# Router logits taken from the residual before it is normed, and the normed rows formed and turned later, in a two-block transformer kernel

## The chip, the cores and the metric

The kernel runs on one core of one Trainium2 chip. The metric is the device time of one execution in microseconds (us), the median of three runs. Engines are called by their names in the profile: PE (TensorE), DVE (VectorE), ACT (ScalarE), POOL (GpSimd) and SP (SyncE, which here only issues transfers).

## What is computed

Two blocks over 512 tokens of width 1024, in float32. The first block is a mixer with three branches, an output projection and a residual, and behind it a mixture of 16 experts in 4 groups. The change touches only the way from the residual to the experts:

```python
h = rms_norm(x, g_norm2) * (1.0 + sc2) + sh2
grp_prob = softmax(h @ w_group + b_group)          # 4 groups
p_g, g_idx = lax.top_k(grp_prob, 1)                # one group for each token
exp_logits = h @ w_router + b_router               # 16 experts
...                                                # two experts of that group, their weights
for gi in range(N_GROUPS):
    act = silu(h @ w_exp_gate[gi]) * (h @ w_exp_up[gi]) * combine[gi]
    y = y + act @ w_exp_down[gi]
```

`rms_norm` scales each token by one factor (rstd); `g_norm2`, `sc2` and `sh2` differ only from feature to feature.

## The kernel before, in words

Activations lie with the features on the 128 partitions and the 512 tokens along them, in KD = 8 blocks `k`. Every product is made exact enough by splitting both sides into a high part (float32r) and the rest: `three` issues the products high by high, low by high and high by low. ACT makes the high part of an activation (`hi_of`, semaphore `hi`), DVE the low part (`lo_of`, semaphore `lo`). Weights come in a stream of pieces of 1 MB, 16 tiles of 128 by 128: SP brings a piece into one of three `raw` slots, POOL splits it into `whi` and `wlo` in four parts, each one copy (L2482) and one difference (L2488), and PE multiplies with it. POOL may split a piece only when PE has ended with the piece two before it, and SP may load a piece only when the piece three before it is split.

The order of each engine is written out by hand in its block of `build`, and one engine waits for another by semaphores. Around the change the program goes:

- The output projection `wout` (4 pieces, 8 outputs). As each output k is ready, DVE adds it to the residual `X[:, k]` (L2059), ACT squares it, and DVE adds the squares up (`add_square`, L1739). PE sums them over the features (`norm_product`, L557), ACT makes `rstd` of it by Ln and Exp (L1231, L1233).
- DVE norms each block into `h2f` (L1755), ACT adds the shift and makes `hhi` (L1248), DVE makes `hlo` (L1725). PE multiplies each block with the router (20 columns: 4 groups and 16 experts, `rhi` and `rlo`), ACT copies the 20 by 512 logits out (`router_T`), PE turns them into tokens by logits (`routerT`, L808).
- DVE works through some 75 small operations on 4 to 80 columns: the group of each token (`grouped`), with the counts of the tokens of each group from PE (`counts`, L817), the order of the groups by size (`ranked`, L2112); then the two experts and their weights, with one Exp on ACT in between (`route_diff`, `route_exp`), the place of each token among those of its group (`places`, PE L822, which sums over the tokens before it), and four masks of 128 by 640 (`in_slot`, L2160). PE multiplies these masks in `slots_filled` (L875), turns the weights (`combT`, L881), and DVE copies them (L2167).
- SP waits for `ranked` before it loads the first expert piece (`moe0`), since the order of the groups says where in the stream it is. PE turns `h2f` into rows of tokens in 8 steps of 4 transposes (`h2_turned`, L801), which ACT copies into `h2_tok` and sends to memory, for a gather some time later.
- The largest group runs first, over all 512 tokens. Each expert has two pieces: `wide_first` multiplies the feature blocks 0 to 3 of it, `wide_second` the blocks 4 to 7. `slots_filled` stands between the two of the first expert. Behind them `expert_weight` spreads the token weights of the expert (L866), ACT copies them and DVE multiplies with them (L2173, L2175); the next expert's fourth PSUM bank comes free only by an operation behind that.

PSUM has 8 banks of 128 by 512. `open_bank` hands out the banks of a group (`main` has six of them, `out` two) in turn and makes PE wait for the reader of what last stood there; `share_banks` gives the groups other banks and starts them at their first.

## Time and profile before

| what | value |
|---|---|
| median of 3 runs | 1885.24 us (1879.75 to 1888.14) |
| the profiled execution, its own time | 1880.21 us |
| its span in the trace | 1878.3 us |
| PE busy, share of the span | 89% |
| POOL, DVE, ACT busy | 54%, 50%, 26% |
| mean granted clock of PE | 0.94 of full speed |

The page gives the busy time of each engine and the chain of waits that ended last. The span is counted from the first to the last instruction that the profiler saw; the time of the execution is 1.9 us longer. The stretch that the change touches lies between 652 us (the end of `wout` on PE) and 726 us (the start of the second expert). Rows of the timeline give the start and the duration of an instruction or of a run of equal ones, and in brackets how long its engine had been idle and what released it. A float32 product shows as two records.

### The profile page before, as it was taken

The page shows a single profiled execution, that of the slowest core. Times are in us where ns is not written, and L with a number is a line of the kernel's source. Part 1 is how long each engine was busy: PE and PEld are TensorE (multiplying, and loading weights), DVE is VectorE, ACT ScalarE, POOL GpSimd, SP SyncE. Part 2 cuts the span into 40 slices and gives each one's busy share as a digit, 9 for nine tenths or more (in the row PEclk, how much of TensorE's full clock was granted, in tenths as well). Part 3 has the DMA queues.
Part 4 walks back from the last instruction along what each step waited for, and adds up shares of the span by engine and source line. Part 5 has one row for each costly group of instructions (what it writes and reads, how often), then busy time and mean ns, then how long its engine had stood idle before and what let it go on. Part 6 is the DMA issues. An engine that isn't in the chain of part 4 may idle for free. (4 is left out here: it accounts for less than half of the span.)

```text
span 1878.3 us, 20749 instructions
## 1 busy us (share of the span) xinstructions
PE 1671.3 (89%) x7778; PEld 1311.7 (70%) x7778; DVE 930.4 (50%) x1437; ACT 496.5 (26%) x939; POOL 1012.1 (54%) x945
## 2 busy tenths in 40 slices
PE   4999798998979979999998699999897699999995
PEld 2778576776757757778876487666574578888884
DVE  7784654498773361231315861865457433133134
ACT  2201322313241121124444422433444420010011
POOL 2767553455717435757870345222374167777772
PEclk8999899998999978999999799998898799999997
DMA  9355211133212032314545532101121013223211
GB/s 362 141 199 197 98 67 68 56 112 113 90 68 90 1 135 93 143 68 157 191 152 187 212 101 90 45 24 45 46 90 68 23 68 105 97 90 112 91 68 45
DMA packets 32694, 197.54 MB, mean 105 GB/s; under 512 B 3735, under 2 KB 7591, under 8 KB 10964
## 3 DMA queue, kind: packets, MB, share of 16 engines
q1 hardware_dynamic: 26040, 179.57, 26.2%
q10 hardware_dynamic: 5836, 14.03, 2.2%
q0 software_dynamic: 720, 2.62, 0.4%
q8 instruction: 63, 1.03, 0.2%
q14 instruction: 35, 0.29, 0.0%
HBM read 190.90 MB, written 7.66 MB: 106 GB/s over the span
## 5 line engine op out<-in xcount | busy, mean ns | idle before, releaser
L2488 POOL TENSOR_TENSOR b_wlo<-b_raw,b_whi 128x512 fp32r<-128x512 f32 x516 | 705.5, 1375 | 70.5 <-ACT b_whi L1507 35.4
L2482 POOL TENSOR_SCALAR b_whi<-b_raw 128x512 fp32r<-128x512 f32 x420 | 312.1, 743 | 760.0 <-PE ps L436 578.2
L434 PE MATMUL ps<-b_hhi,b_whi 128*128 128x512 f32 (+1 forms) x1112 | 450.1, 405 | 27.4 <-POOL b_wlo L2488 8.0
L435 PE MATMUL ps<-b_hlo,b_whi 128*128 128x512 f32 (+1 forms) x1112 | 439.5, 395 | 0.0
L436 PE MATMUL ps<-b_hhi,b_wlo 128*128 128x512 f32 (+1 forms) x1112 | 438.6, 394 | 0.0
L434 PEld LDWEIGHTS ps<-b_hhi,b_whi 128*128 128x128 f32 x1112 | 213.6, 192 | 91.6 <-issue 45.0
L436 PEld LDWEIGHTS ps<-b_hhi,b_wlo 128*128 128x128 f32 x1112 | 213.5, 192 | 45.6
L435 PEld LDWEIGHTS ps<-b_hlo,b_whi 128*128 128x128 f32 x1112 | 213.9, 192 | 44.5 <-issue 2.4
L434 PE MATMUL ps<-b_ahi,b_whi 128*128 128x512 f32 x432 | 176.4, 408 | 12.5 <-DVE b_alo L1721 6.2
L435 PE MATMUL ps<-b_alo,b_whi 128*128 128x512 f32 x432 | 171.6, 397 | 0.0
L436 PE MATMUL ps<-b_ahi,b_wlo 128*128 128x512 f32 x432 | 171.2, 396 | 0.0
L434 PE MATMUL ps<-b_whi,b_hhi 128*128 128x512 f32 (+1 forms) x304 | 117.3, 386 | 14.0 <-DVE b_hlo L1725 5.0
L1255 ACT ACTIVATE b_arena<-ps 128x512 f32<-128x512 f32 (+6 forms) x102 | 54.0, 534 | 258.5 <-PE ps L436 188.5
L435 PE MATMUL ps<-b_wlo,b_hhi 128*128 128x512 f32 (+1 forms) x304 | 115.3, 379 | 0.0
L436 PE MATMUL ps<-b_whi,b_hlo 128*128 128x512 f32 (+1 forms) x304 | 115.3, 379 | 0.0
L434 PEld LDWEIGHTS ps<-b_ahi,b_whi 128*128 128x128 f32 x432 | 83.6, 193 | 39.0 <-DVE b_alo L1721 7.3
L1507 ACT ACTIVATE b_whi<-b_raw 128x512 fp32r<-128x512 f32 x144 | 78.8, 620 | 73.2 <-PE ps L436 70.7
L435 PEld LDWEIGHTS ps<-b_alo,b_whi 128*128 128x128 f32 x432 | 83.4, 193 | 17.9 <-issue 1.2
L436 PEld LDWEIGHTS ps<-b_ahi,b_wlo 128*128 128x128 f32 x432 | 83.1, 192 | 18.0
L434 PEld LDWEIGHTS ps<-b_whi,b_hhi 128*128 128x128 f32 x304 | 58.6, 193 | 25.9 <-issue 14.5
L1246 ACT ACTIVATE b_ahi<-b_arena 128x512 fp32r<-128x512 f32 x52 | 32.8, 632 | 144.1 <-DVE b_arena L2447 106.4
L1255 ACT ACTIVATE b_y<-ps 128x512 f32<-128x512 f32 (+4 forms) x62 | 40.3, 662 | 105.7 <-PE ps L763 91.4
(335 smaller groups left out, 2118.8 us busy)
## 6 DMA issues: line engine op xcount, KB each, us to landing
b_raw<-in_stream SPq DMA_DIRECT2D x165, 1024.0 KB, 4.8
bias_near<-bias_vectors ACTq DMA_DIRECT2D x1, 2298.0 KB
b_x<-in_xT SPq DMA_DIRECT2D x1, 2048.0 KB, 13.1
b_x<-in_xT ACTq DMA_DIRECT2D x1, 2048.0 KB, 7.7
h_tokens<-b_y ACTq DMA_DIRECT2D x1, 2048.0 KB, 11.8
b_arena<-in_cw ACTq DMA_DIRECT2D x1, 2048.0 KB, 7.3
out<-b_x SPq DMA_DIRECT2D x8, 256.0 KB, 2.0
bias_compressed<-bias_vectors ACTq DMA_DIRECT2D x1, 1024.0 KB
```

What stands on the lines that cost most here:

```text
L434: pe.matmul(o, ahi_, bhi_, start=start, stop=False)
L435: pe.matmul(o, ahi_, blo_, start=False, stop=False)
L436: return pe.matmul(o, alo_, bhi_, start=False, stop=stop)
L1246: run(nc.scalar.activation(dst, src, ACT.Copy, scale=gain), "hi")
L1255: run(nc.scalar.activation(dst, src, func, scale=scale, bias=bias), name)
L1507: run(nc.scalar.activation(whi[:, n % SPLIT_SLOTS, c], raw[:, i % RAW_SLOTS, c], ACT.Copy), "moe_hi")
L2482: nc.gpsimd.tensor_scalar(whi[:, s, c], raw[:, r, c], 1.0, 1.0, ALU.mult, ALU.mult)\
L2488: nc.gpsimd.tensor_tensor(wlo[:, s, c], raw[:, r, c], whi[:, s, c].bitcast(F32), ALU.subtract)\
```

## The change

The router's product is linear, and rstd is one factor for a token. So the logits are (X times gain, through the router) times rstd, plus the router's product with the shift `sh2`, which is the same for all tokens. With this:

- `hi_of("route", k)` and `lo_of("route", k)` split X times gain into `ahi` and `alo` as soon as output k of `wout` is added to X, ahead of the squares; PE runs seven of the eight router steps behind `wout`, then the sum of squares, then the eighth. DVE multiplies the logits by rstd as it takes them out of PSUM. `gain` and three small tables are made before the loop.
- The shift's part of the logits is made once, before the attention of the first block: 16 products of one column (`shift`), a diagonal of it by DVE (`route_bias`), and a second product in each of four `routerT` steps adds it.
- DVE does the small operations up to `ranked` and the places first, and then `h2_formed`: the norming and splitting that stood ahead of the router, and the counting table. The choice of experts follows behind it.
- `h2_turned` for the features 0 to 511 of all four token tiles stands ahead of the first piece, for the features 512 to 1023 behind `wide_first`, and `slots_filled` behind `wide_second`. The first piece waits for the low parts of `h2` by blocks. The banks are shared out accordingly. The Exp for `route_diff` stands on ACT behind the last copy of the turned rows.

```diff
@@ -113,3 +113,3 @@
-SPLITS, NSPLITS = offsets({"h1": 8, "ya": 4, "yb": 4, "yc": 4, "merged": 8, "h2": 8,
+SPLITS, NSPLITS = offsets({"h1": 8, "ya": 4, "yb": 4, "yc": 4, "merged": 8, "route": 8, "h2": 8,
                            "moe0": 8, "n0": 8, "conv": 4, "nsa": 4,
@@ -241,2 +241,3 @@
         rout = ar(2560, 512)
+        route_bias = small[0:20, 480:500]
         combT = arena[0:4, 0:512]
@@ -778,2 +779,9 @@
             linear(("gate", 2), range(3), KD, hhi, hlo, 0, "gate_read")
+            pe.wait_ge(sem("router_split"), 1)
+            o = open_bank("shift", "shift_read")
+            for k in range(KD):
+                for n, w in enumerate((rhi, rlo)):
+                    ins = pe.matmul(o[0:20, 0:1], w[:, k, :].bitcast(F32), mod[:, 24 + k:25 + k],
+                                    start=k + n == 0, stop=k + n == KD)
+            mark(ins, "shift")
             pe.wait_ge(sem("rstd_used"), 1 + 4 + 8)
@@ -786,15 +794,19 @@
             linear("wout", range(KD), KD, hhi, hlo, 0, "wout_read", "merged")
+            share_banks(side=[6, 7])
+            logits = open_bank("router", "router_T", "side")
+            def route_step(k):
-            norm_product("sum_h2", KD)
+                pe.wait_ge(sem("lo"), SPLITS["route"] + k + 1)
+                return three(logits[0:20, :], rhi[:, k, :], rlo[:, k, :], ahi[:, k, :], alo[:, k, :],
+                             k == 0, k == KD - 1)
-            o = open_bank("router", "router_T")
-            pe.wait_ge(sem("router_split"), 1)
-            for k in range(KD):
-                pe.wait_ge(sem("lo"), SPLITS["h2"] + k + 1)
-                ins = three(o[0:20, :], rhi[:, k, :], rlo[:, k, :], hhi[:, k, :], hlo[:, k, :], k == 0, k == KD - 1)
-            mark(ins, "router")
+            for k in range(KD - 1):
+                route_step(k)
+            norm_product("sum_h2", KD)
+            mark(route_step(KD - 1), "router")
+            share_banks(main=[0, 1, 2, 3], turned=[4, 5, 6, 7])
             def h2_turned(T, half):
-                o = open_bank(("h2_tok", T, half), "h2_tok")
+                o = open_bank(("h2_tok", T, half), "h2_tok", "turned")
                 for k in range(4):
@@ -803,11 +815,9 @@
-            h2_turned(0, 0)
             pe.wait_ge(sem("router_T"), 1)
+            pe.wait_ge(sem("route_bias"), 1)
             o = open_bank("routerT", "router_read")
             for T in range(ST):
-                ins = pe.transpose(o[:, T * 32:T * 32 + 20], rout[0:20, T * P:(T + 1) * P], ident[0:20, 0:20])
+                pe.matmul(o[:, T * 32:T * 32 + 20], rout[0:20, T * P:(T + 1) * P], ident[0:20, 0:20], start=True, stop=False)
+                ins = pe.matmul(o[:, T * 32:T * 32 + 20], ones[0:20, :], route_bias, start=False, stop=True)
             mark(ins, "routerT")
-            h2_turned(0, 1)
-            h2_turned(1, 0)
-            h2_turned(1, 1)
             goh = small[:, 464:480].rearrange("p (a n) -> p a n", a=ST)
@@ -824,6 +834,5 @@
             mark(ins, "places")
-            for T in range(2, ST):
+            for T in range(ST):
+                pe.wait_ge(sem("lo"), SPLITS["h2"] + 4)
                 h2_turned(T, 0)
-                h2_turned(T, 1)
-            share_banks(turned=[6, 7])
@@ -871,3 +880,3 @@
                 pe.wait_ge(sem("in_slot"), ST)
-                o = open_bank("slots", "slots_known")
+                o = open_bank("slots", "slots_known", "turned")
                 for b in range(5):
@@ -878,3 +887,3 @@
                 pe.wait_ge(sem("combined"), 1)
-                o = open_bank("combT", "combT_read")
+                o = open_bank("combT", "combT_read", "turned")
                 for T in range(ST):
@@ -885,7 +894,11 @@
                 keys = [(("eg", e), 0), (("eg", e), 1), (("eu", e), 0), (("eu", e), 1)]
-                o = wide_first(keys, hhi, hlo, ["silu_read"] * 2 + ["eu_read"] * 2)
+                o = wide_first(keys, hhi, hlo, ["silu_read"] * 2 + ["eu_read"] * 2, None if e else "h2")
                 if e == 0:
-                    slots_filled()
+                    for T in range(ST):
+                        pe.wait_ge(sem("lo"), SPLITS["h2"] + KD)
+                        h2_turned(T, 1)
                 wide_second(o, keys, hhi, hlo)
                 if e == 0:
+                    slots_filled()
+                    share_banks(main=[4, 5, 0, 1, 2, 3], turned=[6, 7])
                     pe.wait_ge(sem("combT_read"), 1)
@@ -1470,8 +1483,5 @@
             for k in range(KD):
-                act.wait_ge(sem("wout_read"), k + 1)
+                hi_of("route", k, ahi[:, k, :], src=X[:, k, :], ready=("wout_read", k + 1), gain=gain[:, k:k + 1])
                 square_for("sum_h2", k, X[:, k, :])
             rstd_of("sum_h2", D)
-            for k in range(KD):
-                hi_of("h2", k, hhi[:, k, :], src=h2f[:, k, :], bias=mod[:, 24 + k:25 + k])
-            evacuate("router", rout[0:20, :], "router_T", src=ps[0:20, bank_of["router"], :])
             act.wait_ge(sem("route_max"), 1)
@@ -1479,8 +1489,14 @@
             run(nc.scalar.activation(gl_e, gl_e, ACT.Exp), "route_exp")
+            def h2_turned(T, half):
+                evacuate(("h2_tok", T, half), h2_tok[:, T, half * 512:(half + 1) * 512], "h2_tok")
+
+            for k in range(KD):
+                hi_of("h2", k, hhi[:, k, :], src=h2f[:, k, :], bias=mod[:, 24 + k:25 + k])
+                if k in (5, 7):
+                    h2_turned(k - 5, 0)
+                    h2_turned(k - 4, 0)
             for T in range(ST):
-                for half in range(2):
-                    evacuate(("h2_tok", T, half), h2_tok[:, T, half * 512:(half + 1) * 512], "h2_tok")
-                if T == 1:
-                    act.wait_ge(sem("route_diff"), 1)
-                    run(nc.scalar.activation(stat[:, 8:12], stat[:, 8:12], ACT.Exp), "route_exp")
+                h2_turned(T, 1)
+            act.wait_ge(sem("route_diff"), 1)
+            run(nc.scalar.activation(stat[:, 8:12], stat[:, 8:12], ACT.Exp), "route_exp")
             act.wait_ge(sem("h2_tok"), 2 * ST)
@@ -2038,2 +2054,6 @@
+            finished(dve, "shift")
+            run(V.tensor_scalar(route_bias, ident[0:20, 0:20], ps[0:20, bank_of["shift"], 0:1], None, ALU.mult),
+                "route_bias")
+            run(V.memset(small[:, 362:363], 0.0), "shift_read")
             dve.wait_ge(sem("bias1_in"), 16 * 4)
@@ -2056,2 +2076,8 @@
             dve.wait_ge(sem("x_in"), 32)
+            run(V.scalar_tensor_tensor(gain[:, :], mod[:, 32:40], 1.0, col("g2", 0, 8), op0=ALU.add, op1=ALU.mult))
+            run(V.tensor_tensor_scan(group4, ones[:, 0:1].to_broadcast([P, 4]), ones[:, 0:1].to_broadcast([P, 4]),
+                                     0.0, ALU.mult, ALU.add))
+            run(V.tensor_scalar(ranks4, group4, -1.0, None, ALU.add))
+            run(V.tensor_scalar(tie4, group4, -1.0, 4.0, ALU.mult, ALU.add))
+            run(V.tensor_scalar(first_w, group4, -1.0, 5.0, ALU.mult, ALU.add))
             for k in range(KD):
@@ -2060,18 +2086,22 @@
                                            op0=ALU.mult, op1=ALU.add), "wout_read")
-                add_squares_behind("sum_h2", k)
-            run(V.scalar_tensor_tensor(gain[:, :], mod[:, 32:40], 1.0, col("g2", 0, 8), op0=ALU.add, op1=ALU.mult))
+                if k >= 2:
+                    add_square("sum_h2", k - 1)
+                lo_of("route", k, alo[:, k, :], ahi[:, k, :], X[:, k, :], gain=gain[:, k:k + 1])
+            add_square("sum_h2", KD - 1)
             wait_rstd()
-            h2_normed = normed(KD, lambda k: X[:, k, :], lambda k: gain[:, k:k + 1])
-            for k in range(KD + 1):
-                if k < KD:
-                    h2_normed(k, h2f[:, k, :])
-                if k:
-                    lo_of("h2", k - 1, hlo[:, k - 1, :], hhi[:, k - 1, :], h2f[:, k - 1, :], mod[:, 23 + k:24 + k])
-            run(V.tensor_tensor_scan(count_up, ones[:, 0:1].to_broadcast([P, SLOTS]), ones[:, 0:1].to_broadcast([P, SLOTS]),
-                                     0.0, ALU.mult, ALU.add))
-            run(V.tensor_tensor(tmp[0][:, 0:P], ident, count_up[:, 0:P], ALU.mult))
-            run(V.tensor_reduce(tok1, tmp[0][:, 0:P], AX.X, ALU.add))
-            run(V.tensor_scalar(ranks4, count_up[:, 0:4], -1.0, None, ALU.add))
-            run(V.tensor_scalar(tie4, count_up[:, 0:4], -1.0, 4.0, ALU.mult, ALU.add))
-            run(V.tensor_scalar(first_w, count_up[:, 0:4], -1.0, 5.0, ALU.mult, ALU.add))
+            finished(dve, "router")
+            run(V.tensor_tensor(rout[0:20, :], ps[0:20, bank_of["router"], :], rstd[0:20, :], ALU.mult), "router_T")
+
+            def h2_formed():
+
+                h2_normed = normed(KD, lambda k: X[:, k, :], lambda k: gain[:, k:k + 1])
+                for k in range(KD + 1):
+                    if k < KD:
+                        h2_normed(k, h2f[:, k, :])
+                    if k:
+                        lo_of("h2", k - 1, hlo[:, k - 1, :], hhi[:, k - 1, :], h2f[:, k - 1, :], mod[:, 23 + k:24 + k])
+                run(V.tensor_tensor_scan(count_up, ones[:, 0:1].to_broadcast([P, SLOTS]), ones[:, 0:1].to_broadcast([P, SLOTS]),
+                                         0.0, ALU.mult, ALU.add))
+                run(V.tensor_tensor(tmp[0][:, 0:P], ident, count_up[:, 0:P], ALU.mult))
+                run(V.tensor_reduce(tok1, tmp[0][:, 0:P], AX.X, ALU.add))
@@ -2112,2 +2142,6 @@
             run(V.tensor_scalar(group_at[:, :], group4, float(MOE_PIECES), None, ALU.mult), "ranked")
+            finished(dve, "places")
+            run(V.tensor_tensor(t16, goh, tiles(bank("places", 16), ST), ALU.mult), "places_read")
+            run(V.tensor_reduce(place_of, t16, AX.X, ALU.add))
+            h2_formed()
@@ -2149,5 +2183,2 @@
             run(V.tensor_reduce(rank_of, t16, AX.X, ALU.add))
-            finished(dve, "places")
-            run(V.tensor_tensor(t16, goh, tiles(bank("places", 16), ST), ALU.mult), "places_read")
-            run(V.tensor_reduce(place_of, t16, AX.X, ALU.add))
             run(V.tensor_scalar(slot_of, rank_of, -1.0, 256.0, ALU.add, ALU.mult))
```

On PE, from the end of `wout` to the first expert piece, before (`b_con` holds the unit matrix, `b_small` the routing values, `b_arena` the squares, `h2f` and the logits):

```order
L436 MATMUL ps<-b_hhi,b_wlo 128x512
L557 MATMUL ps<-b_arena,b_con 128x512 [waits s_wout_read,s_squares_added]
L434 MATMUL ps<-b_hhi,b_rhi 20x512 [waits s_lo,s_router_split,s_wout_read]
...
L808 MATMUL ps<-b_con,b_arena 128x20 [waits s_wout_read,s_router_T]
...
L817 MATMUL ps<-b_small,b_con 128x4 [waits s_router_T,s_grouped]
...
L822 MATMUL ps<-b_small,b_con 128x4 [waits s_h2_tok]
...
L434 MATMUL ps<-b_hhi,b_whi 128x512 [waits s_h2_tok,s_weights_split,s_places_read,s_counts_read]
```

and now (lines of the changed kernel):

```order
L437 MATMUL ps<-b_hhi,b_wlo 128x512
L435 MATMUL ps<-b_ahi,b_rhi 20x512 [waits s_lo,s_dsa_out_read]
...
L558 MATMUL ps<-b_arena,b_con 128x512 [waits s_wout_read,s_squares_added]
...
L820 MATMUL ps<-b_con,b_arena 128x20 [waits s_wout_read,s_route_bias,s_router_T]
L821 MATMUL ps<-b_small,b_con 128x20
...
L827 MATMUL ps<-b_small,b_con 128x4 [waits s_wout_read,s_grouped]
...
L832 MATMUL ps<-b_small,b_con 128x4 [waits s_wout_read]
...
L813 MATMUL ps<-b_con,b_arena 128x128 [waits s_mean_square_read,s_lo]
...
L435 MATMUL ps<-b_hhi,b_whi 128x512 [waits s_places_read,s_weights_split,s_counts_read,s_lo,s_router_read,s_wout_read]
```

The router's steps moved ahead of the sum of squares, and the norming is waited for only by the transposes (L813) and the first piece.

On DVE, around `ranked`, before:

```order
L2112 TENSOR_SCALAR b_group_at<-b_small 128x4 [waits s_dve_step]
L2126 TENSOR_TENSOR b_small<-b_small 128x16 [waits s_ranked]
L2126 TENSOR_TENSOR b_small<-b_small 128x16 [waits s_dve_step]
L2129 TENSOR_TENSOR b_small<-b_small 128x16 [waits s_dve_step]
L2126 TENSOR_TENSOR b_small<-b_small 128x16 [waits s_dve_step]
```

and now:

```order
L2142 TENSOR_SCALAR b_group_at<-b_small 128x4 [waits s_dve_step]
L2144 TENSOR_TENSOR b_small<-b_small,ps 128x16 [waits s_matmuls_done,s_ranked]
L2145 TENSOR_REDUCE b_small<-b_small 128x4 [waits s_places_read]
L1771 SCALAR_TENSOR_TENSOR b_arena<-b_x,b_gain,b_arena 128x512 [waits s_dve_step]
...
L1741 SCALAR_TENSOR_TENSOR b_hlo<-b_arena,b_mod,b_hhi 128x512 [waits s_hi,s_lo]
L2103 SCALAR_TENSOR_TENSOR b_arena<-b_con 128x640 [waits s_lo]
L2105 TENSOR_TENSOR b_arena<-b_con,b_arena 128x128 [waits s_dve_step]
L2106 TENSOR_REDUCE b_small<-b_arena 128x1 [waits s_dve_step]
L2160 TENSOR_TENSOR b_small<-b_small 128x16 [waits s_dve_step] x2
```

Eight norming and eight low-part operations, the table and two small ones now stand between `ranked` and the choice of experts.

## Rows read from the trace of the kernel before

**Rows 1.** The page's busy times: busy us, share, instructions.

```profile
PE 1671.3 (89%) x7778; PEld 1311.7 (70%) x7778; DVE 930.4 (50%) x1437; ACT 496.5 (26%) x939; POOL 1012.1 (54%) x945
```

**Rows 2.** Timeline of PE, 651 to 726 us: start, duration, instruction, idle before.

```profile
651.40 0.39 PE L435 MATMUL ps<-b_hlo,b_whi 128*128 128x512 f32 x1
651.62 0.39 PE L436 MATMUL ps<-b_hhi,b_wlo 128*128 128x512 f32 x1
655.52 2.08 PE L557 MATMUL ps<-b_arena,b_con 128*128 128x512 f32 x2 [3.51 <-DVE b_arena L1739]
...
673.76 1.53 PE L801 MATMUL ps<-b_con,b_arena 128*128 128x128 f32 x12
676.69 1.05 PE L817 MATMUL ps<-b_small,b_con 128*128 128x4 f32 x8 [1.40 <-DVE b_small L2094]
677.60 3.78 PE L822 MATMUL ps<-b_small,b_con 128*128 128x4 f32 x20
681.24 3.65 PE L801 MATMUL ps<-b_con,b_arena 128*128 128x128 f32 x16
689.34 0.77 PE L434 MATMUL ps<-b_hhi,b_whi 128*128 128x512 f32 x1 [4.44 <-POOL b_wlo L2488]
...
703.18 6.30 PE L875 MATMUL ps<-b_small,b_arena 128*128 128x5 f32 x40
...
722.25 1.12 PE L866 MATMUL ps<-b_arena,b_con 4*128 4x512 f32 x2
725.93 0.62 PE L434 MATMUL ps<-b_hhi,b_whi 128*128 128x512 f32 x1 [2.57 <-DVE b_arena L2173]
```

**Rows 3.** Windows: PE, PEld, DVE, ACT, POOL busy (count), granted PE clock, DMA share, GB/s.

```profile
689.00:703.00 14.00, 13.66 (x48) 11.04 (x49) 7.08 (x9) 0.00 (x0) 13.42 (x15) 0.77 0.83 298
```

**Rows 4.** Timeline of DVE, 659 to 711 us.

```profile
659.08 1.54 DVE L1755 SCALAR_TENSOR_TENSOR b_arena<-b_x,b_gain,b_arena 128x512 f32<-128x512 f32 x2 [3.42 <-ACT b_arena L1233]
...
671.84 1.49 DVE L2070 TENSOR_TENSOR_SCAN b_arena<-b_con 128x640 f32<-128x640 f32 x1
...
674.63 0.24 DVE L2082 TENSOR_TENSOR b_small<-ps,b_small 128x80 f32<-128x80 f32 x1
...
679.09 0.17 DVE L2112 TENSOR_SCALAR b_group_at<-b_small 128x4 int32<-128x4 f32 x1
...
684.59 0.16 DVE L2138 TENSOR_TENSOR b_small<-b_small 128x4 f32<-128x4 f32 x1
...
687.36 0.51 DVE L2153 TENSOR_SCALAR b_small<-b_small 128x4 f32<-128x4 f32 x1
...
690.05 4.58 DVE L2160 TENSOR_SCALAR b_arena<-b_arena,b_small 128x640 f32<-128x640 f32 x4
...
710.46 0.68 DVE L2167 COPY b_arena<-ps 4x512 f32<-4x512 f32 x1 [0.47 <-PE ps L881]
```

**Rows 5.** Timeline of POOL: the first part of the first expert piece, and the next.

```profile
687.22 0.62 POOL L2482 TENSOR_SCALAR b_whi<-b_raw 128x512 fp32r<-128x512 f32 x1 [48.05 <-DMA b_raw<-in_stream]
...
689.16 0.61 POOL L2482 TENSOR_SCALAR b_whi<-b_raw 128x512 fp32r<-128x512 f32 x1
```

**Rows 6.** Timeline of DVE at 40 us, the first norming, while POOL splits.

```profile
40.70 0.98 DVE L1755 SCALAR_TENSOR_TENSOR b_arena<-b_x,b_gain,b_arena 128x512 f32<-128x512 f32 x1
41.71 1.65 DVE L1725 SCALAR_TENSOR_TENSOR b_hlo<-b_arena,b_mod,b_hhi 128x512 fp32r<-128x512 f32 x1
43.40 0.99 DVE L1755 SCALAR_TENSOR_TENSOR b_arena<-b_x,b_gain,b_arena 128x512 f32<-128x512 f32 x1
```

**Rows 7.** Timelines around the start of the first attention, and products of one column.

```profile
426.62 0.95 PE L566 MATMUL ps<-b_con,b_x 128*128 128x1 f32 x8
432.70 1.87 PE L566 MATMUL ps<-b_con,b_x 128*128 128x1 f32 x8 [5.13 <-DVE b_x L1780]
...
514.20 1.05 PE L768 MATMUL ps<-b_arena 128*128 128x128 f32 x8
...
519.10 0.29 DVE L2023 SCALAR_TENSOR_TENSOR b_x<-ps,b_x 128x128 f32<-128x128 f32 x1
```

4 lines of the change are left out of this document (2 added, 2 removed).

## The prediction

> **What bounds the kernel now.** I read the page first: PE is busy 89% of the span [rows 1], so the kernel is PE's work plus the holes in it, and a change pays only in a hole. Then the timeline of PE around the change. There the reader sees a stretch with little work: the output projection ends at 651.62 + 0.39 = 652.0 us, the first expert piece starts at 689.34, and what ended the last wait is POOL's split of that piece [rows 2]. POOL in turn was released by the transfer at 687.22 after 48 us without work [rows 5], and SP could ask for the transfer only after `ranked`, which DVE finished at 679.09 + 0.17 = 679.26 [rows 4]. So the chain is: projection, squares, rstd, norming, router, small operations, `ranked`, 7.96 us to the landed piece, 2 us for its first part. Behind it come a first piece at a low clock (granted mean 0.77, so partly at 1.2 instead of 2.4 GHz [rows 3]) and the slots, before which DVE stood idle for long. That last wait is the one to watch: the change gives DVE more to do ahead of the slots.
>
> **The start of the first attention.** The shift product adds 16 products of one column, 32 records. Eight such records with 128 weight columns took 0.95 us right behind dense work and 1.87 us after an idle spell [rows 7], so 3.8 to 7.5 us; these have 20 weight columns, and I take the lower end, since they follow dense work. PE has room: its first logits were issued at 514.20, and DVE first read them at 519.10 [rows 7]. 514.2 + 3.8 = 518.0, and the first logits behind them still come in time. DVE does two small operations more there, 0.35 us, with nothing beside them, so **+0.35**; at the upper end of 7.5 us logits come at about 522, **+3**.
>
> **Up to `ranked`.** The splits of X times gain (for each output one more operation of some 0.78 us on DVE and one on ACT) lie in waits for the projection; without that cover each pair would cost some 1.5. The last of them delays the last addition of squares by nothing: DVE waited there for ACT's square. PE now has 21 router products first, at the 0.22 us of the projection's own rows [rows 2]: 652.0 + 4.7 = 656.7, past 655.52, where the sum of squares started. In return that product meets a warm PE and takes half of its 2.08 us: 657.75 against 657.60 before (658.8 if it is cold). DVE follows 1.48 us behind as before, 659.25; taking out the logits costs what the copy of 4 by 512 costs, 0.68 us [rows 4]; `routerT` is now 16 records at 0.13 (1.05 / 8) to 0.19 us (3.78 / 20) [rows 2], 2.1 to 3.0, say 2.5. DVE gets the logits at 662.6, not at 674.63. From there to `ranked` the work is unchanged, 679.26 - 674.63 = 4.63: **667.2, 12.0 us earlier**. The first piece lands at 667.2 + 7.96 = 675.2.
>
> **What comes behind it now.** DVE waits for the places (PE ends them 681.38 - 674.63 = 6.75 us behind the logits, at 669.4), does two small operations and starts the norming at 669.8. Up to 675.2 it does seven of the 16 operations, 0.78 us each [rows 4]. Then POOL is splitting, and the price of the same pair of operations is in the first norming of the kernel, where POOL was splitting too: 0.98 + 1.65, a pair every 2.70 us [rows 6]. The fourth low part is ready at 677.9, the eighth at 675.2 + 4.5 x 2.7 = 687.4, the table (1.49 [rows 4]) and its two followers at 689.8. PE turns the first halves, 16 transposes in 3.65 us, until 681.6; the first piece takes 703.18 - 689.34 = 13.8 us as before, until 695.4; the second halves cost 1.53 x 16 / 12 = 2.0, until 697.5; the second piece, without the slow start it had, 48 records at 0.225, until **708.3**. There the slots follow. Before they followed the first piece at 703.18.
>
> **DVE's way to the slots.** From 689.8 on it has 27 small operations to the Exp, of which 25 read two operands or are plain scalings, then 14 more, then the masks. Undisturbed one takes (684.59 - 679.09) / 28 = 0.20 us; with POOL splitting, five took 690.05 - 687.36 = 2.69, so 0.54 each [rows 4]. POOL ends its first two pieces at about 694.2 (4.5 parts at 2.7, 3.5 at 1.94 [rows 5]), starts the third at 695.4, when PE is done with the first, and ends it at 703.2. So: 8 operations to 694.2, 6 in the gap, 11 at 0.54 to 701.3, the rest to 701.7; the Exp, behind ACT's last copy, at 702.2; the 14 to 705.6. The masks took 4.58 us while POOL was splitting [rows 4]; POOL now idles until PE ends the second piece at 708.3. No row shows them undisturbed. Upper end 4.58, so 710.2; the lower end is that of the like-sized table step with more work in it, some 0.6 each (1.49 is a running sum over 640), so 708.0. I take the middle, **709.3**: DVE arrives 1 us behind PE.
>
> The Trainium skill (SBUF — State Buffer, § Who interferes with whom) says that a DVE instruction with two SBUF inputs contends with a GpSimd instruction that reads SBUF, and that the one issued second "fully blocks" until the first is done. Read strictly, each small operation waits out a POOL instruction of its own (0.97 us); the row above shows more than one slipping through (0.54). The sum would then be that of rival 2.
>
> **The sum.** From the slots' start to DVE's copy of the weights took 711.14 - 703.18 = 7.96 us, and the spreading product follows 0.1 later: 709.3 + 8.1 = 717.4, and 0.9 more if PE is slow after its wait (0.19 against 0.16 us for 40 records), 718.3, against 722.25: -4.0. The wait of 3.68 us behind it (722.25 to 725.93) stays: the fourth bank again needs DVE's second operation; POOL is idle there, -0.2. PE comes out of a longer sparse stretch into the second expert; the first piece after such a stretch lost (13.8 - 10.8) = 3 us, this one lost less, so +0.6. With the attention: -4.0 - 0.2 + 0.6 + 0.35 = **-3.2 us**. The rest of the program only shifts. Against the profiled execution, 1880.21, that is 1877.0; that execution lies 5 us under the median, so against the median of 1885.24 it gives **1882.0**. A measurement of this kernel tells about 0.5%, 9.4 us, from no change; the three runs before span 8.4 us.
>
> **Rivals.**
> 1. PE ends last, DVE is early (less meeting with POOL, masks at 0.6 each): slots at 708.3 and not slow, -5.9 - 0.2 + 0.6 + 0.35 = -5.1, 1880.1. For it: the masks meet an idle POOL. Against it: 25 of 27 operations of the kind that waited in rows 4. If the first piece also starts warm, 3 us more on PE, DVE again decides.
> 2. DVE waits out a whole POOL instruction each time: 4.5 + 6 + 8 operations by 703.2, the rest free, 705; masks at 708.2 to 712.8, and the spreading product at 721.8: -0.5 + 0.75 = +0.3, 1885.5.
> 3. **Slower**: PE's clock stays at 1.2 GHz through both pieces, because transposes and waits now break up its work three times before the slots. 48 records then cost 20.5 us each time, twice the 0.225: 681.6 + 20.5 + 3.65 + 20.5 = 726.2 and the spreading product at 735: +13, 1898. It decides from about 9 us more of low clock than the 6 us before (each such us loses half). Against it: before, the first piece lost only 3 us to it, right behind just such a sparse stretch.
> 4. The shift products do not fit before the attention: +3 instead of +0.35, 1884.7.
> 5. The routing does not come earlier (the sum of squares or the logits wait for something I missed): only the costs are left, about 1886.
>
> **Numbers.** Forecast 0.40, rival 1 0.25, rival 2 0.14, rival 3 0.05, rival 4 0.08, rival 5 0.08. Faster by over 0.5% needs rival 1 with a warm start and masks in time, or scatter of the runs: 0.09. Slower by over 0.5% is rival 3 nearly alone: 0.04. The rest, 0.87, is within 0.5%. The range takes in the forecast and rivals 1, 2, 4 and 5 with the scatter of a median: 1875 to 1889.
>
> **What would show it.** Right: `ranked` near 667, POOL's first part near 675, norming operations of 1.0 and 1.65 us on DVE, the first expert piece on PE near 682, a wait of about 1 us for DVE's masks ahead of the slots, the spreading product near 718. Wrong: `ranked` later than 671 (rival 5), DVE's masks done before PE's second piece (rival 1) or 4 us behind it (rival 2), a granted clock near 0.5 from 682 to 708 (rival 3), DVE idle ahead of its first attention operation (rival 4).

## The result, and the profile after

| | before | changed |
|---|---|---|
| median of nine runs each | 1885.24 us (1879.75 to 1888.8) | 1892.43 us (1884.3 to 1896.88) |
| ratio to before, 95% interval | | 1.0042 (1.0025 to 1.0059) |
| the profiled execution, its own time | 1880.21 us | 1884.3 us |
| its span | 1878.3 us | 1882.1 us |

The change makes the kernel slower, by 0.42% (4.7 to 11.1 us by the interval). That is still inside the 0.5% that I called no change, but it is measured, it has the other sign than the forecast of -3.2 us, and the median lies outside the range of 1875 to 1889.

The page of the changed kernel, which answers to [rows 1]:

```profile
span 1882.1 us, 20872 instructions
...
PE 1670.1 (89%) x7822; PEld 1316.3 (70%) x7822; DVE 950.7 (51%) x1449; ACT 501.6 (27%) x946; POOL 1016.0 (54%) x945
```

The busy times hardly differ, so the loss is in idle time and order. The timeline of PE over the same stretch, answering to [rows 2]:

```profile
656.33 1.02 PE L558 MATMUL ps<-b_arena,b_con 128*128 128x512 f32 x2
...
664.44 1.87 PE L827 MATMUL ps<-b_small,b_con 128*128 128x4 f32 x8 [2.17 <-DVE b_small L2124]
666.17 4.41 PE L832 MATMUL ps<-b_small,b_con 128*128 128x4 f32 x20
679.70 3.68 PE L813 MATMUL ps<-b_con,b_arena 128*128 128x128 f32 x16 [9.12 <-DVE b_hlo L1741]
683.02 0.78 PE L435 MATMUL ps<-b_hhi,b_whi 128*128 128x512 f32 x1
...
694.70 1.91 PE L813 MATMUL ps<-b_con,b_arena 128*128 128x128 f32 x16
...
707.15 0.39 PE L437 MATMUL ps<-b_hhi,b_wlo 128*128 128x512 f32 x1
715.12 8.70 PE L884 MATMUL ps<-b_small,b_arena 128*128 128x5 f32 x40 [7.59 <-DVE b_arena L2191]
723.68 1.01 PE L890 MATMUL ps<-b_con,b_small 128*4 128x128 f32 x4
725.53 2.07 PE L875 MATMUL ps<-b_arena,b_con 4*128 4x512 f32 x2 [0.84 <-DVE b_arena L2198]
730.01 0.76 PE L435 MATMUL ps<-b_hhi,b_whi 128*128 128x512 f32 x1 [2.41 <-DVE b_arena L2204]
```

The row at 715.12 is the one to see. PE ended the second piece at 707.5 (forecast: 708.3) and then stood 7.59 us for DVE's masks; before, the slots had no wait at all. The windows (columns: PE busy, granted clock, DMA share, GB/s) show the second part of the price:

```profile
683.00:697.00 14.00, 14.00 (x69) 0.95 0.23 75
697.00:715.00 18.00, 10.54 (x47) 0.91 0.60 234
715.00:730.00 15.00, 11.64 (x46) 0.50 0.18 70
```

Behind that wait the granted clock is 0.50, the lower level of 1.2 GHz. The first piece and the turns behind it in return run at 0.95, against 0.77 for the first piece in [rows 3]. The timeline of DVE, answering to [rows 4]:

```profile
667.66 0.17 DVE L2142 TENSOR_SCALAR b_group_at<-b_small 128x4 int32<-128x4 f32 x1
670.69 0.17 DVE L2144 TENSOR_TENSOR b_small<-b_small,ps 128x16 f32<-128x16 f32 x1 [2.86 <-PE ps L832]
...
671.10 1.54 DVE L1771 SCALAR_TENSOR_TENSOR b_arena<-b_x,b_gain,b_arena 128x512 f32<-128x512 f32 x2
...
678.66 0.98 DVE L1741 SCALAR_TENSOR_TENSOR b_hlo<-b_arena,b_mod,b_hhi 128x512 fp32r<-128x512 f32 x1
679.68 1.65 DVE L1771 SCALAR_TENSOR_TENSOR b_arena<-b_x,b_gain,b_arena 128x512 f32<-128x512 f32 x1
...
689.50 1.78 DVE L2103 TENSOR_TENSOR_SCAN b_arena<-b_con 128x640 f32<-128x640 f32 x1
...
695.26 1.14 DVE L2160 TENSOR_TENSOR b_small<-b_small 128x16 f32<-128x16 f32 x1
696.44 0.54 DVE L2163 TENSOR_TENSOR b_small<-b_small 128x16 f32<-128x16 f32 x1
697.02 0.17 DVE L2166 TENSOR_REDUCE b_small<-b_small 128x4 f32<-128x16 f32 x1
...
706.20 0.17 DVE L2175 TENSOR_SCALAR b_small<-b_small 128x4 f32<-128x4 f32 x1 [0.34 <-ACT b_small L1501]
...
708.57 1.11 DVE L2186 SCALAR_TENSOR_TENSOR b_small<-b_small 128x4 f32<-128x4 f32 x1
709.72 0.56 DVE L2187 TENSOR_SCALAR b_small<-b_small 128x4 f32<-128x4 f32 x1
710.31 0.17 DVE L2188 COPY b_small<-b_small 128x16 f32<-128x16 f32 x1
710.52 4.54 DVE L2191 TENSOR_SCALAR b_arena<-b_arena,b_small 128x640 f32<-128x640 f32 x4
```

And that of POOL, answering to [rows 5]: the first part of the first piece, parts of the third (696.34) and the fourth piece (from 707.70).

```profile
675.80 0.62 POOL L2513 TENSOR_SCALAR b_whi<-b_raw 128x512 fp32r<-128x512 f32 x1 [36.37 <-DMA b_raw<-in_stream]
...
695.08 1.29 POOL L2519 TENSOR_TENSOR b_wlo<-b_raw,b_whi 128x512 fp32r<-128x512 f32 x1
696.34 0.62 POOL L2513 TENSOR_SCALAR b_whi<-b_raw 128x512 fp32r<-128x512 f32 x1
697.04 1.30 POOL L2519 TENSOR_TENSOR b_wlo<-b_raw,b_whi 128x512 fp32r<-128x512 f32 x1
...
707.70 0.62 POOL L2513 TENSOR_SCALAR b_whi<-b_raw 128x512 fp32r<-128x512 f32 x1 [3.48 <-PE ps L437]
708.40 1.26 POOL L2519 TENSOR_TENSOR b_wlo<-b_raw,b_whi 128x512 fp32r<-128x512 f32 x1
```

Read the two together at 695 to 697. The small operation of 1.14 us ends with POOL's difference (695.08 + 1.29), the next, of 0.54, with POOL's copy (696.34 + 0.62), and the third takes its bare 0.17. A POOL part of 1.96 us lets three of DVE's small operations pass. The same meeting stretches the masks at 710.52 to 1.14 us each: POOL could start its fourth piece at 707.70, because PE had just ended with the second.

So the 11.4 us that `ranked` came earlier (667.83 against 679.26) shrink to 6.3 at the first piece (683.0 against 689.34), because the forming of h2 now stands behind `ranked` and meets POOL from 675.80 on, and turn into a loss of 4.1 at the second expert (730.01 against 725.93).

### The profile page after: what moved, and what is told of

The parts are those of the page before. It is cut to its first block and busy times, and to the rows that moved or that the text cites. A ratio compares the mean times of both kernels' runs of the same rounds, so it can differ in the third digit from the quotient of the medians.

```text
span 1882.1 us, 20872 instructions
## 1 busy us (share of the span) xinstructions
PE 1670.1 (89%) x7822; PEld 1316.3 (70%) x7822; DVE 950.7 (51%) x1449; ACT 501.6 (27%) x946; POOL 1016.0 (54%) x945
## 5 line engine op out<-in xcount | busy, mean ns | idle before, releaser
L435 PE MATMUL ps<-b_whi,b_hhi 128*128 128x512 f32 (+1 forms) x304 | 116.9, 384 | 13.4 <-DVE b_hlo L1741 5.3
L1268 ACT ACTIVATE b_arena<-ps 128x512 f32<-128x512 f32 (+5 forms) x101 | 53.3, 534 | 243.2 <-PE ps L437 160.2
```

Source lines behind the costliest of these rows:

```text
L435: pe.matmul(o, ahi_, bhi_, start=start, stop=False)
L1268: run(nc.scalar.activation(dst, src, func, scale=scale, bias=bias), name)
```

## The experiments

Single executions of one kernel scatter by some 15 us here, and much of that arises long before the stretch in question. The thirteen traces fall into two groups: in seven the granted clock between 300 and 350 us is 0.93 and `wout` ends at 650 to 652 us (the early group), in six the clock there is 0.66 to 0.69 and `wout` ends at 661 to 667 (the late group). So each run is given in two ways: by its ratio to the kernel before, and by landmarks of its trace, in us behind the end of `wout` on PE (651.6 us in the changed kernel, 652.0 before). "Spreading" is the product L875 (before: L866) of the first expert, "second spreading" that of the second expert, "end" the end of the trace.

| kernel | `ranked` | first piece | masks start | slots | spreading | second expert | second spreading | end | ratio (95%) |
|---|---|---|---|---|---|---|---|---|---|
| before | 27.2 | 37.3 | 38.0 | 51.2 | 70.2 | 73.9 | 97.5 | 1226.3 | 1 |
| forecast for the change | 15.2 | 29.6 | 53.6 | 57.3 | 66.3 | 69.8 | | | 0.998 |
| changed | 16.2 | 31.4 | 58.9 | 63.5 | 73.9 | 78.4 | 103.0 | 1230.5 | 1.0042 (1.0025 to 1.0059) |
| c1 changed, again | 15.9 | 30.7 | 58.7 | 63.3 | 73.7 | 78.2 | 103.0 | 1229.8 | 1.0036 (1.0016 to 1.0057) |
| c2 fourth piece held | 16.1 | 31.3 | 57.4 | 59.8 | 69.8 | 74.3 | 97.7 | 1222.7 | 1.0026 (1.0010 to 1.0041) |
| c3 third piece held | 16.1 | 31.4 | 52.2 | 55.7 | 61.9 | 66.4 | 90.3 | 1220.2 | 0.9979 (0.9957 to 1.0001) |
| c11 c3 again | 16.0 | 31.1 | 52.0 | 55.7 | 61.7 | 66.2 | 90.2 | 1219.5 | 0.9969 (0.9953 to 0.9985) |
| c4 filler products | 15.9 | 31.0 | 58.9 | 63.5 | 70.5 | 75.0 | 99.8 | 1227.3 | 1.0004 (0.9979 to 1.0028) |
| c5 c3 and banks | 16.0 | 30.9 | 52.2 | 55.5 | 61.8 | 63.8 | 87.4 | 1216.0 | 0.9953 (0.9931 to 0.9975) |
| c10 c5 again | 16.1 | 31.3 | 52.2 | 55.8 | 62.0 | 64.0 | 87.4 | 1216.0 | 0.9948 (0.9925 to 0.9971) |
| c6 c5, first piece held | 16.0 | 29.7 | 52.4 | 55.1 | 61.4 | 63.4 | 87.2 | 1215.7 | 0.9978 (0.9956 to 0.9999) |
| c7 choice first | 16.0 | 47.0 | 60.0 | 70.6 | 77.8 | 82.3 | 106.8 | 1236.4 | 1.0064 (1.0036 to 1.0092) |
| c8 slots between | 16.0 | 31.2 | 57.2 | 59.6 | 82.3 | 86.0 | 108.0 | 1232.9 | 1.0077 (1.0048 to 1.0106) |
| c9 before, banks | 27.2 | 37.4 | 38.1 | 51.2 | 70.3 | 71.4 | 93.3 | 1222.6 | 0.9989 (0.9972 to 1.0007) |

c1 to c4 ran on one chip, c5 to c8 on one, c9 to c11 on one, each with its own runs of the kernel before. The landmarks and the end repeat to 0.7 us or better (changed and c1, c3 and c11, c5 and c10), although each of these pairs has one trace from each group. The end can differ by some 4 us from what the second spreading product promises: c2 has that product 0.2 us behind the kernel before, and its end 3.6 us ahead. The ratios depend as well on how many executions fall into which group, and c2's says 0.26% slower. A few us in a ratio alone, or in one landmark alone, carry no weight below.

**c1: the changed kernel once more.**

> The changed kernel once more, as the control of the others on the same chip. Both theories: 0.3 to 0.6% slower than before, PE idle for 6 to 9 us ahead of the slots, the slots' 40 records at 0.19 to 0.23 us each.

It measured 1.0036 (1.0016 to 1.0057), with a wait of 7.58 us and 0.22 us a record, and the landmarks stand. The slowdown is real.

**c2 and c3: POOL held back.** One line in POOL's block makes it wait for the four masks before it splits a piece, the fourth in c2 (`MOE_AT + 3`), the third in c3 (`MOE_AT + 2`):

```diff
+                if i == MOE_AT + 3:
+                    pool.wait_ge(sem("in_slot"), ST)
                 if rank == 0:
                     pool.wait_ge(sem(f"raw_in{r}"), 16 * (i // RAW_SLOTS + 1))
```

> The changed kernel with POOL held off the fourth expert piece until the four masks are made. Theory A (DVE is late at the slots because its operations meet POOL's split): the masks take 0.6 us each instead of 1.14, the five small operations ahead of them 0.2 instead of 0.5, and the slots start near 711.5 instead of 715.1, so 3 to 4 us off the changed kernel. Theory B (the loss comes from what was added ahead of the slots, whatever POOL does): the slots start within 1 us of 715. Theory C (the loss is PE's clock, which the sparse stretch lets fall): the start may move, but the time moves by less than 1.5 us.

> The changed kernel with POOL held off the third and the fourth expert piece until the masks are made. Theory A: from 695 us on DVE works alone, its remaining small operations take 0.2 us each, the masks are ready at 705 to 706, ahead of PE's second piece (707.4), the slots start at 707.5, the spreading product near 716, and the kernel is 8 to 12 us faster than the changed one and 3 to 6 us faster than before. The third piece is then split at about 713, in time for the second expert. Theory B: no gain. Theory C: a gain of at most what the wait was at low clock, 4 us.

The masks (DVE) and the slots and what follows (PE) in c2's timeline:

```profile
708.88 2.32 DVE L2191 TENSOR_SCALAR b_arena<-b_arena,b_small 128x640 f32<-128x640 f32 x4
```

```profile
711.25 8.31 PE L884 MATMUL ps<-b_small,b_arena 128*128 128x5 f32 x40 [3.88 <-DVE b_arena L2191]
```

and in c3's:

```profile
702.94 2.32 DVE L2191 TENSOR_SCALAR b_arena<-b_arena,b_small 128x640 f32<-128x640 f32 x4
```

```profile
706.45 4.52 PE L884 MATMUL ps<-b_small,b_arena 128*128 128x5 f32 x40
710.83 0.95 PE L890 MATMUL ps<-b_con,b_small 128*4 128x128 f32 x4
712.62 2.07 PE L875 MATMUL ps<-b_arena,b_con 4*128 4x512 f32 x2 [0.84 <-DVE b_arena L2198]
```

With POOL quiet a mask takes 0.58 us instead of 1.14. Holding the fourth piece brings the slots 3.7 us forward, holding the third 7.8. PE then doesn't wait for them, its granted clock is still 0.99 during them, and 40 slot products take 4.52 us instead of 8.70. The second expert comes 12.0 us earlier than in the changed kernel, and the end 10.3, with the same work done. By the ratios c3 is 0.57% faster than c1, while c2's ratio (1.0026) can't be told from c1's. That carries the theory that DVE comes late because its operations meet POOL's, and speaks against a loss from the added work as such. The Trainium skill (SBUF — State Buffer, § Who interferes with whom) names both kinds of DVE instruction that contend with GpSimd, those with two SBUF inputs and `tensor_scalar` in a 2-port mode; the masks are `tensor_scalar`, and 0.58 against 1.14 us agrees that they contend; no run shows the mode that they ran in.

**c4: is it the clock?** 30 needless products on PE fill its wait for the masks (the first of the added waits makes sure that bank 7 has been read):

```diff
+                pe.wait_ge(sem("h2_tok"), 2 * ST)
+                for n in range(30):
+                    pe.matmul(ps[:, 7, :], hhi[:, n % KD, 0:P], hhi[:, n % KD, :], start=True, stop=True)
                 pe.wait_ge(sem("in_slot"), ST)
```

> The changed kernel with 30 needless products of 128 by 512 ahead of the wait for the masks, so that PE works through 6.5 of its 7.6 idle us; they write a free PSUM bank and leave the result alone. Theory A: the start of the slots stays at 715; what is won is the clock alone, 40 records at 0.16 instead of 0.22 us (2.4 us) and a warmer start of the second expert (up to 1.7 us), so 2 to 4 us faster than the changed kernel. Theory C (the clock is the whole loss): 7 us or more, as fast as before or faster. If the clock plays no part: within 1 us of the changed kernel.

```profile
718.25 6.96 PE L882 MATMUL ps<-b_hhi 128*128 128x512 f32 x30
726.10 5.28 PE L887 MATMUL ps<-b_small,b_arena 128*128 128x5 f32 x40 [0.89 <-DVE b_arena L2194]
731.24 1.01 PE L893 MATMUL ps<-b_con,b_small 128*4 128x128 f32 x4
```

The slots come as late as in the changed kernel (63.5), but take 5.28 us instead of 8.70, so the way from them to the spreading product falls from 10.4 to 7.0 us. The second expert comes 3.4 us earlier and the end 3.2. So the low clock behind the wait is worth 3.4 us of the change's loss, as theory A had it; the 7.6 us of the wait itself stay.

**c5: the hole behind the spreading product.** c3 still waits 2.48 us for DVE ahead of the second expert. c5 is c3 with another order of banks:

```diff
-                    share_banks(main=[4, 5, 0, 1, 2, 3], turned=[6, 7])
+                    share_banks(main=[4, 5, 3, 0, 1, 2], turned=[6, 7])
```

> The changed kernel with POOL held back before the third expert piece until the masks are written (as in c3), and with the six banks behind the slots handed out as 4, 5, 3, 0, 1, 2 instead of 4, 5, 0, 1, 2, 3, so that the fourth bank of the second expert is one that DVE reads with its first operation (L2204), not its second. c3's trace shows 712.62 for the spreading product, 2.07 us of it, and 717.16 for the second expert with a wait of 2.48 us that ended with DVE's second L2204. Theory E (that wait is only the order in which banks come free): the second expert starts about 2.0 to 2.5 us earlier against the end of the output projection, some 64 instead of 66.4, and keeps the gain at the spreading product of its second weight (some 88 instead of 90.3); ratio to the kernel before about 0.9967. Rival F (the second expert then waits elsewhere: for another bank that ACT reads, or its pieces come late because POOL was held back): the start or the next spreading product stays where c3 has it, ratio 0.998. If the clock of PE also stays up for want of the gap, 1 us more: c3 shows 1.6 times the usual duration for some 4 us behind the gap.

The second expert follows right behind the product, 2.0 us after its start, at 63.8, where theory E wanted some 64. The clock did not stay up: the next products take 0.63 us a record, as in c3.

```profile
722.78 2.07 PE L875 MATMUL ps<-b_arena,b_con 4*128 4x512 f32 x2 [1.21 <-DVE b_arena L2198]
724.79 0.80 PE L435 MATMUL ps<-b_hhi,b_whi 128*128 128x512 f32 x1
725.38 0.63 PE L436 MATMUL ps<-b_hlo,b_whi 128*128 128x512 f32 x1
```

**c6: the first piece held too**, until the fourth low part of h2 is ready.

```diff
+                if i == MOE_AT:
+                    pool.wait_ge(sem("lo"), SPLITS["h2"] + 4)
```

> c5 with one wait more: POOL starts the first expert piece only when DVE has made the fourth low part of h2. In the changed kernel POOL starts at 675.80, while DVE forms h2 at 2.70 us a pair, and the first half turn on PE waits 9.12 us for DVE, until 679.70; the piece is wanted at 683. Theory A (meeting POOL is what slows DVE here too): the fourth low part comes about 1 us earlier, at 15 to 16 us behind ranked less that, PE's first half turns and its first piece start 0.5 to 1 us earlier, since POOL's first part (1.95 to 2.7 us) is then ready about when the turns end; the end gains up to 1 us over c5. Rival G: POOL's first part comes late instead (DVE's fifth and sixth block meet it all the same), and PE waits for POOL at the first piece: first piece later by up to 1 us, the end the same or worse. I hold G for as likely as A here: what is at stake is 1 us either way.

The fourth low part comes at 26.4 instead of 27.5 us (c5), the first piece 1.2 us earlier than in c5, the second expert 0.4, the end 0.3. So theory A's mechanism is there, and little of it reaches the end. The ratio is higher than c5's, 0.9978 against 0.9953, with intervals that overlap; in its profiled run `wout` ends at 666.9 us against c5's 661.0, ahead of anything that differs. Differences of 0.3 to 0.4 us are below what the pairs above repeat to, so whether anything remains is open.

**c7: the choice of experts ahead of the forming.** `h2_formed()` is called behind the computation of `slot_of`, and ACT's second Exp stands ahead of its `hi_of("h2", ...)`.

```diff
             run(V.tensor_reduce(place_of, t16, AX.X, ALU.add))
-            h2_formed()
...
             run(V.scalar_tensor_tensor(slot_of, rank_of, 0.0, slot_of, op0=ALU.is_gt, op1=ALU.mult))
+            h2_formed()
```

> The changed kernel with DVE's choice of the two experts and their weights (some 40 small operations) moved from behind the forming of h2 to ahead of it, and ACT's second Exp likewise; POOL is not held back. Before the first piece lands, POOL is idle, and the small operations then take 0.2 us instead of 0.54 to 0.65, some 8 to 9 us in all. The forming then starts near 680 instead of 671, under POOL from its start: fourth low part about 691, so PE's first piece starts some 8 us later against the end of the projection (39 to 41 instead of 31.4), the first piece ends at 54, and the slots follow the second piece at 67 to 68 with no wait for the masks. Theory A (it is DVE's operations under POOL that come late, and the order of DVE's work decides which engine pays): PE waits at the first piece instead of at the slots, the second expert starts at 77 to 80 (after: 78.4), and the ratio is within 0.2% of the changed kernel's. Rival H (the place of the wait matters: with the wait ahead of the first piece PE runs both pieces and the slots without a break at full clock): second expert at 74 to 76, ratio about 0.2% below the changed kernel's.

The wait did move to the first piece, and grew. DVE's timeline shows the price of a small operation without POOL and with it:

```profile
682.04 0.17 DVE L2151 TENSOR_SCALAR b_small<-b_small 128x4 f32<-128x4 f32 x1
682.24 0.17 DVE L2153 TENSOR_TENSOR b_small<-b_small 128x4 f32<-128x4 f32 x1
...
689.65 1.12 DVE L2179 TENSOR_TENSOR b_small<-b_small 128x16 f32<-128x16 f32 x1
690.81 0.54 DVE L2180 TENSOR_TENSOR b_small<-b_small 128x16 f32<-128x16 f32 x1
```

and PE's the wait:

```profile
704.86 3.29 PE L813 MATMUL ps<-b_con,b_arena 128*128 128x128 f32 x16 [25.21 <-DVE b_hlo L1741]
```

POOL began at 684.91, before the choice was through, and the forming, from 693.51 on, met it from its start: first piece at 47.0, not at 39 to 41, second expert 3.9 us later than in the changed kernel (82.3, where theory A wanted 77 to 80 and rival H 74 to 76). As an order this one loses. One half of rival H came true all the same: with the wait ahead of the first piece, PE went from that piece to the second expert in 35.3 us, as in c3 (35.0) and not in the changed kernel's 47.0. What cost the time is that the first piece came 15.6 us later, more than the 11.7 gained behind it. Whether a wait of equal length would be cheaper there was not tested.

**c8: one part undone.** The slots stand between the two pieces again, as before the change.

```diff
+                if e == 0:
+                    slots_filled()
                 wide_second(o, keys, hhi, hlo)
                 if e == 0:
-                    slots_filled()
```

> The changed kernel with the slots back where they stood before, behind the first piece (and the second half turns) and ahead of the second piece: one part of the change undone. The masks can't be ready for it: PE stands at the slots from about 697.5. POOL then can't start the fourth piece, since PE still has the second piece to do, so DVE's last operations and the masks meet only the third piece, which POOL ends near 704. Theory A: the masks are done at about 709 to 710 instead of 715.1, the slots run at a low clock behind a wait of 12 us until 719, the second piece takes 11 to 14 us behind them, and the second expert starts at 83 to 85 behind the end of the projection (after: 78.4): slower than the changed kernel by 5 to 7 us, ratio to the kernel before 1.006 to 1.008. Rival B (the loss was in moving the slots, not in DVE's lateness): second expert at or before 76, ratio at or below 1.001.

```profile
711.69 8.70 PE L884 MATMUL ps<-b_small,b_arena 128*128 128x5 f32 x40 [14.60 <-DVE b_arena L2192]
```

PE waits 14.60 us there, twice as long as in the changed kernel, and the second expert comes 7.6 us later, a little more than expected (86.0 against 83 to 85); at the end 2.4 us of it are left. With the choice of experts behind the forming, moving the slots back was right. The masks end at 59.5, and not at 63.4, since POOL has no fourth piece to split, as in c2.

**c9: the bank order on the kernel before**, for what is left of early routing.

```diff
                 if e == 0:
+                    first4 = [bank_of[key] for key in keys]
+                    share_banks(main=[bank_of["slots"], bank_of["combT"]] + first4)
                     pe.wait_ge(sem("combT_read"), 1)
```

> The kernel before with only the order of banks of c5: from the spreading product on, main hands out the bank of the slots, the bank of the turned weights and then the four of the first expert, so that the second expert's fourth bank needs only DVE's first operation. In the kernel before PE waited 2.57 us there (722.25 spreading product, 725.93 second expert). Theory E (that hole is a matter of bank order in either kernel): the second expert starts near 71.5 behind the end of the output projection instead of 73.9, ratio about 0.9987. Theory E alone would then leave c5 (63.8) some 7 to 8 us ahead of this kernel, and that is what early routing is worth once POOL is held back. Rival F (the hole is filled by another wait): second expert at 73 or later, ratio 1.000.

```profile
720.42 1.12 PE L866 MATMUL ps<-b_arena,b_con 4*128 4x512 f32 x2
743.45 1.12 PE L866 MATMUL ps<-b_arena,b_con 4*128 4x512 f32 x2
```

The hole closes in this kernel too (71.4 instead of 73.9; 23.0 us from one spreading product to the next). The ratio of 0.9989 alone can't be told from 1. POOL was not held back in the kernel before; its slots have no wait for DVE that this could shorten (703.18 in [rows 2]).

**c10 and c11: c5 and c3 again, on c9's chip.**

> c5 once more, on the chip of c9, so that the two can be set side by side. Landmarks as in c5: masks 52.2, slots 55.5, spreading product 61.8, second expert 63.8 behind the end of the projection; that is 10.1 us ahead of the kernel before at the second expert, so a ratio near 0.9947; c5 measured 0.9953. Against c9 7 to 8 us, 0.4%.

> c3 once more, on the chip of c9 and c10. By its landmarks (second expert at 66.4, 7.5 us ahead of the kernel before) the ratio should be 0.9960; c3 measured 0.9979 with an interval of 0.9957 to 1.0001. If the landmarks are what counts, this one falls between c9 and c10, some 2.5 us behind c10; if it comes out at 0.998 again, some 4 us of what the landmarks show are lost in a part of the program that I have not looked at.

Medians on that chip: before 1883.98, c9 1881.48, c11 1877.04, c10 1870.8 us. The order is that of the landmarks. c11 measured 0.9969, between the 0.9960 of its landmarks and the 0.998 of the other reading, and lies 6.2 us behind c10 in the medians, 3.5 us at the end and 2.2 at the second expert. c10 beats the kernel before by 0.52% (0.29 to 0.75%) and c9 by 10.7 us in the medians, 7.7 us by the two ratios, 7.4 us at the second expert, 6.6 us at the end. So early routing is worth some 7 us, once POOL keeps out of DVE's way; in the change as made that worth was spent on a wait.

## Why the prediction was wrong

**Up to the second piece it held**, to within 2 us or so. `ranked` 667.83 (667.2), POOL's first part 675.80 (675.2), norming operations of 1.65 and 0.98 us, first piece at 683.0 (681.6), end of the second piece at 707.5 (708.3). The last match has luck in it: the first piece began 1.4 us late and took 11.7 us instead of the 13.8 "as before", at a granted clock of 0.95. The counts and places ran slower, 0.23 us a record against [rows 2]'s 0.13 and 0.19, which made the forming start 1.3 us late. The shift product cost nothing that shows: DVE's first attention operation starts at 519.02, against 519.10 in [rows 7]. The trace of the changed kernel has its 32 records in a microsecond, and attention begins 0.5 us behind [rows 7]'s 514.20, still well ahead of DVE:

```profile
513.81 0.21 PE L784 MATMUL ps<-b_mod,b_rhi 128*20 128x1 f32 x2
...
514.58 0.19 PE L784 MATMUL ps<-b_mod,b_rlo 128*20 128x1 f32 x2
514.70 1.16 PE L769 MATMUL ps<-b_arena 128*128 128x128 f32 x8
```

My 3.8 us came from products with 128 weight columns and was too high by a factor of four. Rivals 4 and 5 are out, and so is rival 3: the stretch from 683 to 697 ran at 0.95, the next, with the second piece, at 0.91.

**The step that failed is "DVE's way to the slots".** It put the end of the masks at 709.3; they ended at 715.06, 5.8 us later. By its own terms:

| term | forecast | measured | late by |
|---|---|---|---|
| table done (places, forming, scan) | 689.8 | 692.83 | 3.0 |
| 27 small operations and the Exp | 12.4 us | 13.4 us (to 706.20) | 1.0 |
| 14 operations to the masks | 3.4 us | 4.3 us (to 710.52) | 0.9 |
| the masks | 3.7 us | 4.5 us | 0.8 |

The first two, 4.0 us together, are mis-sized. Of the 3.0 us, 1.3 are the late start of the forming, 0.8 the forming itself and 1.0 the table, whose operations POOL stretched (1.78 us for the running sum, 1.49 in [rows 4]). Of the small operations each cost 0.65 us under POOL, where five rows of [rows 4] gave 0.54, and the gap of 1.2 us between POOL's second and third piece, in which six of them were to run at 0.2, didn't come: POOL ended the second piece at 696.37 instead of 694.2 and went straight on with the third. c3 against c2 prices the meeting with that third piece: the masks start at 52.2 instead of 57.4.

The last two, 1.7 us, are a wrong premise. I let POOL idle until PE ended the second piece at 708.3, which was right to 0.6 us, and then had DVE nearly through by then. Being 4 us late, DVE met the fourth piece with its last small operations and all four masks. A delay of DVE there feeds on itself, and c2 prices this last meeting: 3.7 us at the slots. (The forecast had part of that in it already, by its middle price for the masks.) The prediction held both ends for the masks (0.6 and 1.15 each) and took the middle, although they are all or nothing: 0.58 in c2, 1.14 here. I watched the right wait and gave DVE 1 us behind PE where it was 7.6.

**The clock behind the wait was mis-sized.** "0.9 more if PE is slow" was taken from 0.16 and 0.19 us a record, which for 40 records already make 1.2. At the lower clock of this stretch a slot product took 0.22 us, and the way from the slots to the spreading product 10.4 us instead of 9.0; c4 shows 7.0 with PE kept busy. Together: 5.8 + 1.4 = 7.2 us at the spreading product (725.53 against 718.3), which itself then took 2.07 us instead of [rows 2]'s 1.12 and so made the next hole 1 us longer. That is 8.2 us in all at the second expert: 4.1 later than before the change, where the steps of the sum had 4.1 earlier. The sum's +0.6 for a colder second expert measured 1.0 (24.6 us from its start to its spreading product, 23.6 before).

**Rival 2 was right in part of its mechanism.** It had DVE wait out a POOL instruction each time, at 0.97 us an operation, and the masks end at 712.8; it got 0.14. The trace shows that of three small operations two do wait out a POOL instruction each, and the third slips in between, which makes 0.65 us, nearer to the forecast's 0.54 than to rival 2's price. The 0.54 of [rows 4] is the same pattern, read over five operations of which two slip in. And rival 2 let the rest run free from 703.2 and so missed the fourth piece, as the forecast did. No rival held the case that came, a kernel clearly slower by a wait for DVE: the chance of slower was given nearly whole to rival 3, the clock, with 0.05, and belonged to the masks.

**What stays open.** The landmarks give +4.5 us at the second expert and +5.5 at its spreading product, the two ratios +7.9 and +6.8 us. From the end of `wout` to the end of the trace the changed kernel took 4.2 us longer than the kernel before, and c1 3.5, so what the ratios show beyond that does not sit later in the program. It may be scatter (the intervals reach down to 4.7 and 3.0), or it arises ahead of the end of `wout`, where the traces fall into two groups. Only two traces show the old order of the routing (before, c9), both from the early group; whether the change makes the late group more frequent or more costly, no run tells.

## What to carry to other kernels

An engine that is idle ahead of a wait is only slack until the change moves work into it: add up that engine's way to the wait under the contention that it will meet there, and ask at each end whether the other side has started its next piece. Where two engines slow each other down, a one-line wait on the one with slack (POOL here, 12 us at the second expert) can be worth more than the reordering itself (some 7 us here). And a two-valued price, met or not met, goes into the sum at one of its values, with the point in time from which it flips.

## What the runs showed of the hardware

Products of one column with 20 weight columns took about 0.03 us a record (32 in 0.96 us), against 0.12 with 128 columns in [rows 7]; no run varies the weight columns alone. DVE's reductions showed 0.17 us also in the middle of a POOL instruction (at 703.10, in POOL's difference of 702.93, and in c7 at 691.59, in that of 691.41), where their neighbours of two operands took 0.54 to 1.14. And 30 products whose result nobody reads made the 40 slot products behind them 3.4 us shorter.
